# Two attention blocks placed head by head inside the projections that feed them

## The chip, the cores and the metric

One core of a Trainium2 chip. The metric is the device time of one execution in microseconds, the median of the runs shown. The kernel is written engine by engine: TensorE (PE) multiplies, VectorE (DVE), ScalarE (ACT) and GpSimd (POOL) work on elements, and SyncE (SP) issues the loads. Engines meet only at semaphores.

## What is computed

A transformer of three layers on 256 tokens of width 1024, in fp32. The change touches only the mixing part of the first layer:

```python
h = rms_norm(x, norm1_g[l])
parts = jnp.split(h @ w_in[l], list(SPLIT_POINTS), axis=-1)   # 2064 + 4608 columns
gq, gk, gv, gr, ga_lr = parts[:5]
log_a = jax.nn.log_sigmoid((ga_lr @ w_gla_a2[l] + b_gla_a[l]).astype(jnp.float32)) / GLA_TAU
o_gla = gla_chunked(heads(gq, GLA_DK), heads(gk, GLA_DK), heads(gv, GLA_DV), heads(log_a, GLA_DK))
o_gla = rms_norm(o_gla, gla_out_norm_g[l]).reshape(B, S, GLA_V_W) * jax.nn.silu(gr.astype(jnp.float32))
y_gla = o_gla.astype(x.dtype) @ w_proj_gla[l]
for gi, (window, dilation) in enumerate(DIL_PATTERNS):        # 3 groups, 4 heads of 128
    q, k, v = parts[5 + 3 * gi: 8 + 3 * gi]
    q = rms_norm(heads(q, DIL_DH), dil_q_norm_g[l, gi])
    k = rms_norm(heads(k, DIL_DH), dil_k_norm_g[l, gi])
    o_g, m_g, d_g = dilated_group(q, k, heads(v, DIL_DH), slopes[gi], window, dilation)
...
y_att = o_att.reshape(B, S, DIL_W).astype(x.dtype) @ w_proj_attn[l]
g_gla, g_att = jnp.split(jax.nn.sigmoid(h @ w_branch_gate[l] + b_branch_gate[l]), 2, axis=-1)
x = x + ((g_gla * y_gla + g_att * y_att) @ w_out[l]).astype(x.dtype)
```

GLA is a gated linear attention in chunks of 16 tokens with a running 128x128 state per head (4 heads, 16 chunks). The dilated attention is a softmax over three groups with different dilations. A mixture of 32 experts closes the first layer; two further layers follow.

## The kernel before, in words

**Stages.** The program is a list `stages` (from line 3217). Each stage gives every engine a function and ends at a barrier of all four (`end_stage`, line 439). The stages around the change are: norm `n1`, projection `in_a` (2064 columns: GLA's q, k, v, gate, and 16 decay columns last), `gla_*` (lines 959 to 1128), projection `in_b` (4608 columns), `dil_*` (1152 to 1274), projection `gates`, `y_gla`, `y_att` with the sum `sum_dve` (3173), a turn of the result, and `out_1`.

**Projections.** Weights stream in pieces of 128 x 2048 floats (1 MB) through a ring of nine slots (`stream`, 460, on SP's queue). ScalarE casts a piece to its rounded upper part (`split_high`, 554), VectorE subtracts to get the lower part (`split_low`, 560), and TensorE runs three matmuls per product of parts (`matmul3`, 536). A block of 512 columns is two pieces. Each piece is used for both tiles of 128 tokens, 24 matmuls of 512 columns in all; the y projections need one piece a block. `pe_project` (570) cycles through four PSUM banks, and `evacuate` (592) copies each finished tile out, on ScalarE for in_a and in_b, on VectorE for the others. Upper parts have four buffers. `pe_project` and `evacuate` have hooks, points at which a stage can put other work between pieces or between the two tiles of a piece; later layers use them.

**GLA stage.** Transposes of q and k of all heads, decay logits, logarithm and cumulative sums for all heads at once (1024 wide), scores, and then for each head and tile (`COMBOS`) a product of keys with masked values (`kv`, 985; POOL makes the 1024-wide masked values at 1126), a serial chain of state updates on VectorE (1100), and 16-column matmuls for the output (1005). Norm, gate and a turn for all heads end it.

**Dilated stage.** Squares, norms and scaling of q and k for all heads first (1225 to 1239), then head by head: 12 transposes (1160), scores (1167, 1169), bias, mask and maximum on VectorE (1250 to 1263), exponentials on ScalarE (1213, 1214), 9 transposes of the probabilities (1174, 1178), 9 matmuls with the values (1184, 1187), a division (1268).

Masks are built on VectorE between pieces of in_a (`masks_between`, 836), and rotary tables at its end (`rope_dve`, `rope_act`, called at 918 and in `params_wait`).

Of the kernel before, what the change touches and what calls it, by code (L numbers as in the profile page):

```python
# [117 lines left out]
def emit(nc, d, out):  # L118
    ctx = ExitStack()
    with ctx:  # L120
# [73 lines left out]
        gla_og = MT.take(GD)  # L194
        gla_a2 = MT.take(GW)[0:RANK]
# [29 lines left out]
        count_steps("gla_tensor", {"gla_turned": 3, "gla_logit": 1, "gla_scores": 1, "gla_ke_turned": 1,  # L225
                                   "gla_o_turned": 1, "gla_out": 1})
        count_steps("gla_scalar", {"gla_lr": 1, "gla_ln": 1, "gla_exp": 3, "gla_ke": 1, "gla_oT": 1, "gla_silu": 1,
                                   "gla_sq": 1, "gla_rt": 1, "gla_ogT": 1})
        count_steps("gla_vector", {"gla_y": 1, "gla_cum": 2, "gla_scaled": 1, "gla_att": 1, "gla_ms": 1, "gla_gated": 1})
# [43 lines left out]
        def new_piece(copies, group=None):  # L273
# [7 lines left out]
            p.copies = [(ring_flat[:, p.slot * PIECE + a:p.slot * PIECE + b], src) for a, b, src in copies]  # L281
            p.size = max(b for _, b, _ in copies)
# [6 lines left out]
        def project(name, weight, kc, width, engines, group, first=0, chunked=False):  # L289


            pieces_of[name], jobs_of[name] = [], []
            rows = weight.rearrange("(c p) n -> p c n" if chunked else "(p c) n -> p c n", c=kc)

            def jobs(p, col, n, off):
                for t in range(NT):
                    e = engines[len(jobs_of[name]) % len(engines)]
                    order[e] += 1
                    j = Job(t, col, n, off, e, order[e], len(jobs_of[name]))
                    p.jobs.append(j)  # L300
                    jobs_of[name].append(j)
# [10 lines left out]
            blocks = [(c0, min(512, width - c0)) for c0 in starts]  # L312
            if kc == PLE // P:
                p = new_piece([(0, PIECE, rows)], group)
                p.c0, p.chunks, p.width, p.last = 0, kc, width, True
                for c0, n in blocks:
                    jobs(p, c0, n, c0)
# [3 lines left out]
            for c0, n in blocks:  # L321
                chunks = kc if kc * n <= PIECE else kc // 2
                for c in range(0, kc, chunks):
                    p = new_piece([(0, chunks * n, rows[:, c:c + chunks, c0:c0 + n])], group)
                    p.c0, p.chunks, p.width, p.last = c, chunks, n, c + chunks == kc
                    pieces_of[name].append(p)
                    if c == 0:
                        jobs(p, c0, n, 0)
# [83 lines left out]
        group_a, group_b, group_c = [Group(4) for _ in range(3)]  # L412
        project("in_a", d["w_in"][0][:, 0:ZA], KC, ZA, ["act"], group_a)
        n_first = order["piece"]
        project("in_b", d["w_in"][0][:, ZA:ZA + ZB], KC, ZB, ["act"], group_b)
        project("gates", d["w_branch_gate"][0], KC, 2 * D, ["dve"], group_c)
        project("y_gla", d["w_proj_gla"][0], GW // P, D, ["dve"], group_c)
        project("y_att", d["w_proj_attn"][0], GW // P, D, ["dve"], group_c)
        project("out_1", d["w_out"][0], KC, D, ["dve"], group_c)
# [40 lines left out]
        def stream(sp, pieces):  # L460
            for p in pieces:
                if p.n >= RAW:
                    sp.wait_ge(used, p.n - RAW + 1)
                for dst, src in p.copies:
                    sp.dma_start(dst.rearrange("p (c n) -> p c n", n=src.shape[2]), src).then_inc(piece_ready[p.slot], 16)
# [104 lines left out]
        def pe_project(pe, name, xT, hook=None):  # L570
            hi, lo = xT
            jobs = jobs_of[name]
            for p in pieces_of[name]:
                pe.wait_ge(split, p.k)
                a, b = high_of(p, p.width), low_of(p, p.width)
                for j in p.jobs:
                    if p.c0 == 0 and j.q >= 4:
                        e = jobs[j.q - 4]
                        pe.wait_ge(evac_act if e.engine == "act" else evac_dve, e.evac)
                    cols, tok = slice(j.off, j.off + j.n), slice(j.tile * P, (j.tile + 1) * P)  # L580
                    for i in range(p.chunks):
                        c = p.c0 + i
                        mm = matmul3(pe, ps[:, j.q % 4, 0:j.n], hi[:, c, tok], lo[:, c, tok], a[:, i, cols], b[:, i, cols],
# [8 lines left out]
        def evacuate(eng, name, engine, copy=None, between=None, norm=None, hook=None):  # L592
# [7 lines left out]
            for i, p in enumerate(pieces_of[name]):  # L600
# [3 lines left out]
                if hook:  # L604
                    hook(eng, i, 0)
                for j in p.jobs if p.last else []:
                    if j.engine == engine:
# [3 lines left out]
                        copy(j, ps[:, j.q % 4, 0:j.n]).then_inc(evac_act if engine == "act" else evac_dve, 1)  # L611
                if hook:
                    hook(eng, i, 1)
# [134 lines left out]

        P1_LOADS = [
# [2603 lines left out]
```

## Time and profile before

| | us |
|---|---|
| median of 3 runs | 2638.46 (2633.21 to 2642.4) |
| the profiled execution | 2638.94 |
| its span, first to last instruction | 2637.2 |
| TensorE busy | 2360.6 (90%), mean clock 0.941 |
| VectorE busy | 1838.0 (70%) |
| ScalarE busy | 1451.2 (55%) |
| GpSimd busy | 56.5 (2%) |
| DMA | 617.66 MB, 234 GB/s on the mean |

The page cuts the span into 40 slices of 66 us. In the line of TensorE the first eight digits are 7, 6, 8, 9, 4, 6, 8, 7 where most others are 9, and the DMA line shows 0 in two of these slices. The mean over the span says little about this part; the windows by stage are the view to open.

### The profile page before, as it was taken

The numbers are of one execution on the slowest core, as the hardware profiler recorded it, in microseconds if no ns is written. First come the engines' busy times: TensorE is split into PE (matmuls) and PEld (weight loads), VectorE is DVE, ScalarE is ACT, GpSimd is POOL, SyncE is SP. The second block draws the span as 40 slices with busy tenths as digits, with TensorE's granted clock in tenths as the row PEclk, the third lists the DMA queues.
The fourth block names the chain that finished last, engine by engine and source line by source line (L and its number), as shares of the span: only waits on it lengthen the run. The fifth ranks groups of instructions, "written<-read, shape, count | busy, mean of one in ns | idle before, by whom it ended". The sixth has DMA issues, their size and how long they took to land. (4 is left out here: it accounts for less than half of the span.)

```text
span 2637.2 us, 30476 instructions
## 1 busy us (share of the span) xinstructions
PE 2360.6 (90%) x12398; PEld 1920.6 (73%) x12398; DVE 1838.0 (70%) x1869; ACT 1451.2 (55%) x1357; POOL 56.5 (2%) x47
## 2 busy tenths in 40 slices
PE   7689468799999999797899989779999999999996
PEld 6567356678888888676688768557888888888884
DVE  5443544588888898476555447657888888888884
ACT  4243123477777777443534444346767767767763
POOL 0200000000000000011000001000000000000000
PEclk9789678899999999898999999889999999999997
DMA  7025024399999999630555444127999998999990
GB/s 261 32 99 188 0 74 136 110 345 367 359 368 356 368 357 370 208 105 19 162 175 192 166 130 142 33 72 279 363 358 357 366 361 291 363 357 357 367 327 29
DMA packets 232601, 617.66 MB, mean 234 GB/s; under 512 B 23289, under 2 KB 68729, under 8 KB 194817
## 3 DMA queue, kind: packets, MB, share of 16 engines
q1 hardware_dynamic: 231056, 611.39, 65.4%
q10 hardware_dynamic: 1392, 4.19, 0.4%
q8 instruction: 102, 1.67, 0.2%
q14 instruction: 51, 0.41, 0.1%
HBM read 612.40 MB, written 1.05 MB: 233 GB/s over the span
## 5 line engine op out<-in xcount | busy, mean ns | idle before, releaser
L562 DVE TENSOR_TENSOR ring_parts<-ring,high_parts 128x2048 fp32r<-128x2048 f32 x574 | 1282.1, 2274 | 219.6 <-ACT high_parts L558 198.6
L558 ACT CAST high_parts<-ring 128x2048 fp32r<-128x2048 f32 x574 | 1078.5, 1897 | 259.7 <-PE ps L540 226.1
L540 PE MATMUL ps<-high_parts,arena_parts 128*128 128x512 f32 (+2 forms) x1560 | 620.4, 398 | 0.0
L538 PE MATMUL ps<-high_parts,hT_parts 128*128 128x512 f32 (+2 forms) x1120 | 451.9, 403 | 38.8 <-DVEq L442 23.5
L539 PE MATMUL ps<-ring_parts,hT_parts 128*128 128x512 f32 (+2 forms) x1120 | 445.2, 397 | 0.0
L538 PE MATMUL ps<-high_parts 128*128 128x512 f32 x912 | 365.4, 401 | 0.0
L539 PE MATMUL ps<-ring_parts,high_parts 128*128 128x512 f32 x912 | 359.2, 394 | 0.0
L540 PE MATMUL ps<-high_parts 128*128 128x512 f32 x912 | 356.6, 391 | 0.0
L540 PEld LDWEIGHTS ps<-high_parts,arena_parts 128*128 128x128 f32 x1560 | 299.3, 192 | 69.1
L538 PE MATMUL ps<-high_parts,arena_parts 128*128 128x512 f32 x744 | 295.4, 397 | 11.7 <-ACTq L442 4.5
L539 PE MATMUL ps<-ring_parts,arena_parts 128*128 128x512 f32 x744 | 294.0, 395 | 0.0
L538 PEld LDWEIGHTS ps<-high_parts,hT_parts 128*128 128x128 f32 x1120 | 216.7, 194 | 90.3 <-DVEq L442 26.0
L539 PEld LDWEIGHTS ps<-ring_parts,hT_parts 128*128 128x128 f32 x1120 | 216.9, 194 | 49.6 <-issue 0.2
L540 PEld LDWEIGHTS ps<-high_parts 128*128 128x128 f32 x912 | 171.5, 188 | 41.8
L538 PEld LDWEIGHTS ps<-high_parts 128*128 128x128 f32 x912 | 172.1, 189 | 37.5
L539 PEld LDWEIGHTS ps<-ring_parts,high_parts 128*128 128x128 f32 x912 | 171.0, 188 | 35.7
L538 PEld LDWEIGHTS ps<-high_parts,arena_parts 128*128 128x128 f32 x744 | 140.8, 189 | 46.0 <-ACTq L442 4.9
L539 PEld LDWEIGHTS ps<-ring_parts,arena_parts 128*128 128x128 f32 x744 | 141.0, 190 | 32.5
L2075 DVE SCALAR_TENSOR_TENSOR arena<-ps,arena 128x512 f32<-128x512 f32 x80 | 57.8, 722 | 149.3 <-PE ps L540 134.1
L1991 ACT CAST arena_parts<-ps 128x512 fp32r<-128x512 f32 x80 | 45.4, 567 | 140.4 <-PE ps L1889 140.4
L540 PE MATMUL ps<-high_parts,hT_parts 128*128 128x512 f32 x304 | 120.5, 397 | 0.0
L2009 ACT ACTIVATE arena<-ps 128x512 f32<-128x512 f32 x80 | 46.2, 578 | 68.6 <-PE ps L540 68.6
(523 smaller groups left out, 1867.4 us busy)
## 6 DMA issues: line engine op xcount, KB each, us to landing
ring<-in_moe_w SPq DMA_DIRECT2D x248, 1024.0 KB, 5.5
ring<-in_w_gate SPq DMA_DIRECT2D x64, 1024.0 KB, 5.3
ring<-in_w_up SPq DMA_DIRECT2D x64, 1024.0 KB, 5.2
ring<-in_w_down SPq DMA_DIRECT2D x64, 1024.0 KB, 5.2
ring<-in_w_in SPq DMA_DIRECT2D x46, 1024.0 KB, 4.9
ring<-in_ffn_w SPq DMA_DIRECT2D x44, 512.0 KB, 4.8
ring<-in_moe_w SPq DMA_DIRECT2D x32, 512.0 KB, 5.0
ring<-in_w_out SPq DMA_DIRECT2D x12, 1024.0 KB, 4.9
```

What stands on the lines that cost most here:

```text
L538: pe.matmul(dst, a_hi, b_hi, start=first, stop=False, skip_group_check=True)
L539: pe.matmul(dst, a_hi, b_lo, start=False, stop=False, skip_group_check=True)
L540: return pe.matmul(dst, a_lo, b_hi, start=False, stop=last, skip_group_check=True)
L558: act.copy(high_flat(p), raw_flat(p)).then_inc(upper, 1)
L562: dve.tensor_tensor(raw_flat(p, ring_parts_flat), raw_flat(p), f32(high_flat(p)), ALU.subtract).then_inc(split, 1)
L1991: act.copy(m_hidT[:, 0:st.n // P, :].rearrange("p c n -> p (c n)"), ps[:, TURN, 0:st.n])\
L2009: act.activation(m_sg[:, 0:st.n], ps[:, GATE, 0:st.n], ACT.Silu).then_inc(sig("moe_silu"), 1)
L2075: dve.scalar_tensor_tensor(out=m_hid[:, 0:st.n], in0=src, scalar=m_gate[:, q:q + 1], in1=m_sg[:, 0:st.n], op0=ALU.mult, op1=ALU.mult).then ...
```

## The change

The two projections in_a and in_b become one, `in_ab`. Its blocks are the 16 decay columns first, then four blocks that each hold q, k, v and gate of one GLA head, then nine blocks with the dilated columns ordered by head (q and k of the three groups, then v). A piece of such a block is loaded by one copy for each 128 columns. in_ab, gates, y_gla and y_att form one stage. They use two PSUM banks in turn (0 and 1), which leaves six for attention, and three buffers of upper parts. The attention steps hang on hooks at fixed slots; slot 2p is behind the first tile of piece p, slot 2p + 1 behind the second. The lists G_TURN to D_PV name the slots.

Smaller changes: state products work on two halves of 64 rows with masked values 512 wide; output norm and gate are computed per head on transposed data, with the sum of squares by a matmul with ones; the silu is built from an exponential and a reciprocal; bias and mask are added up ahead and a single instruction does addition and minimum; the probabilities are turned by a matmul with a diagonal of 1/sum; the sigmoid is a tanh, with its 1/2 applied in `out_copy`; some masks are made earlier; the rotary tables move to piece 31.

```diff
+        for what, engine in (("turned", "tensor"), ("scores", "tensor"), ("hi", "scalar"), ("lo", "vector")):
+            count_steps(f"{what}_{engine}", {f"g_{what}": GH, f"d_{what}": DH})
...
+                    j.bank = len(lanes[name]) % banks
+                    j.before = lanes[name][-banks] if len(lanes[name]) >= banks else None
...
-                    p = new_piece([(0, chunks * n, rows[:, c:c + chunks, c0:c0 + n])], group)
+                    p = new_piece([(0, chunks * n, rows[:, c:c + chunks, c0:c0 + m], n, at) for (c0, m), at in zip(part, places)], group)
...
-        group_a, group_b, group_c = [Group(4) for _ in range(3)]
-        project("in_a", d["w_in"][0][:, 0:ZA], KC, ZA, ["act"], group_a)
...
+        group_m = Group(3)
+        in_blocks = [[(4 * GW, RANK)]] + [[(k * GW + h * GD, GD) for k in range(4)] for h in range(GH)]
+        dil_cols = [(ZA + (3 * g + k) * GW + h * DD, DD) for h in range(DH)
+                    for k, g in [(k, g) for g in range(DG) for k in range(2)] + [(2, g) for g in range(DG)]]
+        in_blocks += [dil_cols[i:i + 4] for i in range(0, len(dil_cols), 4)]
+        project("in_ab", d["w_in"][0], KC, ZA + ZB, ["act"], group_m, blocks=in_blocks, banks=2)
+        project("gates", d["w_branch_gate"][0], KC, 2 * D, ["dve"], group_m, banks=2, after="in_ab")
...
-                    if p.c0 == 0 and j.q >= 4:
-                        e = jobs[j.q - 4]
+                    if p.c0 == 0 and j.before:
+                        e = j.before
                         pe.wait_ge(evac_act if e.engine == "act" else evac_dve, e.evac)
...
+        G_TURN, G_SCORES, G_KV, G_OUT, G_MS = [[a + 4 * h for h in range(GH)] for a in (8, 10, 12, 15, 17)]
+        D_TURN, D_SCORES, D_PTURN, D_PV = [28, 37, 46, 57], [31, 40, 49, 60], [34, 43, 52, 64], [37, 46, 55, 67]
...
+            def gla_kv(h):
+                pe.wait_ge(sig("g_att"), h + 1)
+                if h:
+                    pe.wait_ge(sig("g_state"), h)
+                for t in range(NT):
+                    pe.wait_ge(sig("g_vm"), NT * h + t + 1)
+                    for f in range(2):
+                        rows = slice(64 * f, 64 * f + 64)
+                        mm = pe.matmul(bank(4 + 2 * t + f), g_ke[rows, t, :], g_vm[rows, t].rearrange("p n v -> p (n v)"),
+                                       start=True, stop=True)
+                mm.then_inc(sig("g_kv"), 1)
+
+            def gla_out(h):
+                pe.wait_ge(sig("g_state"), h + 1)
+                if h:
+                    pe.wait_ge(sig("g_og"), h)
...
+            def dil_turn(h):
+                pe.wait_ge(sig("d_normed"), h + 1)
...
+        def first_act(act):
+            def logit_act():
+                act.wait_ge(*ended("g_logit", 1))
...
+                astep(act, act.activation(flat(g_abs), flat(g_abs), ACT.Exp, scale=-1.0))
+                act.activation(flat(g_abs), flat(g_abs), ACT.Ln, bias=1.0).then_inc(sig("g_ln"), 1)
...
+            def hook(act, i, phase):
...
+                    if i == 2:
+                        logit_act()
...
+                    if i == 31:
+                        rope_act(act)
+                    return
+                if i == 3:
+                    decay_act()
...
+                    if i == G_MS[h] // 2:
+                        act.wait_ge(sig("g_ms"), h + 1)
+                        act.activation(g_e, ps[:, 2, S:2 * S], ACT.Sqrt, scale=1.0 / GD, bias=eps_c).then_inc(sig("g_rt"), 1)
...
+            def gla_states(h):
+                dve.wait_ge(sig("g_kv"), h + 1)
+                for n in range(NT * NCH - 1):
...
+            def gla_silu(h):
+                dve.wait_ge(sig("g_sq"), h + 1)
+                vstep(dve, dve.tensor_scalar(g_e, g_e, 1.0, None, ALU.add))
+                vstep(dve, dve.reciprocal(g_e, g_e))
...
+            def gla_gate(h):
+                dve.wait_ge(sig("g_rt"), h + 1)
+                vstep(dve, dve.reciprocal(g_e, g_e))
...
+            def dil_squares(h):
+                after_block(dve, keys_block(h))
...
+                vstep(dve, dve.tensor_tensor(d_sq[h], qk, qk, ALU.mult))
+                dve.tensor_reduce(d_ss, d_sq[h], AX, ALU.add).then_inc(sig("d_ms"), 1)
...
+            def dil_max(h):
+                dve.wait_ge(*ended("d_scores", h + 1))
+                dve.tensor_tensor_reduce(out=d_s[:, 0:DG * P].rearrange("p (g n) -> p g n", g=DG),
...
+        def first_mix_pool(pool):
+            for h in range(GH):
+                after_block(pool, 1 + h)
...
+                    pool.tensor_tensor(g_vm[:, t], g_za[h][:, 2, t, :].unsqueeze(1).to_broadcast([P, 4, GD]),
...
+        def out_copy(dve, j, src):
+
+            cols = x[:, j.tile, j.col:j.col + j.n]
+            return dve.scalar_tensor_tensor(out=cols, in0=src, scalar=0.5, in1=cols, op0=ALU.mult, op1=ALU.add)
...
+            (first_pe, first_act, first_dve, first_mix_pool),
             stage_turn("ym", c_y, low_1),
...
-            stream(sp, pieces_of["in_a"][0:6])
+            stream(sp, pieces_of["in_ab"][0:3])
+            for dst, src in G_LOADS:
+                sp.dma_start(dst, src).then_inc(sig("g_params"), 16)
+            stream(sp, pieces_of["in_ab"][3:7])
```

`keys_block(h)` is the block with which the last of a dilated head's q and k arrive (6, 8, 10 and 13); VectorE squares them at piece 12, 16, 20 and 26 and normalizes at the next.

## Rows read from the trace of the kernel before

**Rows 1.** Windows by stage: length; PE, PEld, DVE, ACT, POOL busy us; clock; DMA share; GB/s.

```profile
17.20:72.60 55.40, 55.34 (x240) 45.86 (x240) 31.91 (x101) 20.03 (x22) 0.00 (x0) 0.90 0.70 226
72.60:153.70 81.10, 46.01 (x235) 35.02 (x235) 42.47 (x86) 23.75 (x26) 15.08 (x8) 0.71 0.04 14
153.70:258.30 104.60, 103.77 (x432) 83.03 (x432) 38.83 (x18) 43.73 (x35) 0.00 (x0) 0.97 0.52 171
258.30:367.90 109.60, 44.52 (x212) 39.24 (x212) 54.66 (x92) 22.27 (x41) 0.00 (x0) 0.67 0.03 10
```

**Rows 2.** Timeline of VectorE, last sums: start us, us, engine, line, operation.

```profile
445.02 2.36 DVE L3176 TENSOR_TENSOR arena<-arena 128x1024 f32<-128x1024 f32 x2
```

**Rows 3.** Timeline of ScalarE and VectorE in the in_b projection.

```profile
176.22 0.69 ACT L3182 ACTIVATE arena<-ps,rstd 128x512 f32<-128x512 f32 x1 [0.83 <-PE ps L540]
...
179.62 1.89 ACT L558 CAST high_parts<-ring 128x2048 fp32r<-128x2048 f32 x1
...
187.45 0.69 ACT L3182 ACTIVATE arena<-ps,rstd 128x512 f32<-128x512 f32 x1 [0.85 <-PE ps L540]
...
175.42 2.29 DVE L562 TENSOR_TENSOR ring_parts<-ring,high_parts 128x2048 fp32r<-128x2048 f32 x1 [2.80 <-ACT high_parts L558]
```

**Rows 4.** Timeline of TensorE, the 48 matmuls of the 16-column block.

```profile
64.73 0.17 PE L538 MATMUL ps<-high_parts,hT_parts 128*128 128x16 f32 x1
...
67.32 0.35 PE L538 MATMUL ps<-high_parts,hT_parts 128*128 128x16 f32 x1
...
72.21 0.36 PE L540 MATMUL ps<-high_parts,arena_parts 128*128 128x16 f32 x1
```

**Rows 5.** Windows after the restart of TensorE at 153.7.

```profile
156.00:160.00 4.00, 4.00 (x12) 3.17 (x11) 4.00 (x2) 3.17 (x2) 0.00 (x0) 0.56 0.00 0
160.00:164.00 4.00, 4.00 (x19) 3.21 (x18) 2.37 (x2) 1.73 (x1) 0.00 (x0) 1.00 0.17 35
```

**Rows 6.** Timeline of TensorE, the second dilated head.

```profile
303.25 1.47 PE L1160 MATMUL ps<-ident,arena 128*128 128x128 f32 x12
306.13 0.91 PE L1167 MATMUL ps<-arena 128*128 128x128 f32 x6 [1.41 <-ACT arena L1210]
306.88 1.46 PE L1169 MATMUL ps<-arena 128*128 128x256 f32 x6
```

**Rows 7.** Timeline of TensorE in the GLA stage.

```profile
120.64 1.96 PE L991 MATMUL ps<-arena 128*128 128x512 f32 x4
...
126.39 1.63 PE L1005 MATMUL ps<-arena 128*128 128x16 f32 x14
```

**Rows 8.** Timeline of TensorE, 64-row matmuls in a later layer.

```profile
1130.98 0.48 PE L2344 MATMUL ps<-arena 64*128 64x256 f32 x1
1130.99 0.48 PE L2345 MATMUL ps<-arena 64*128 64x256 f32 x1
1131.30 0.38 PE L2344 MATMUL ps<-arena 64*128 64x256 f32 x1
```

**Rows 9.** Timeline of VectorE in the GLA and dilated stages.

```profile
83.39 1.66 DVE L1057 TENSOR_SCALAR arena<-ps,gla_bT 128x256 f32<-128x256 f32 x4 [3.36 <-PE ps L971]
...
109.45 5.54 DVE L1100 SCALAR_TENSOR_TENSOR arena<-arena,ps 128x128 f32<-128x128 f32 x14
...
258.26 1.23 DVE L1228 TENSOR_TENSOR arena<-arena 128x1024 f32<-128x1024 f32 x1 [18.37 <-ACTq L442]
```

**Rows 10.** Groups of VectorE, reciprocals: count, busy us, mean ns.

```profile
L3058 DVE RECIPROCAL arena<-arena 128x60 f32<-128x60 f32 x2 | 1.1, 528 | 0.1
...
L1233 DVE RECIPROCAL arena<-arena 128x48 f32<-128x48 f32 x1 | 0.5, 452 | 0.3 <-ACT arena L1203 0.3
```

**Rows 11.** DMA over 1261 to 1400, loads of 1 KB rows: GB/s in 40 slices.

```profile
GB/s 164 365 405 348 257 78 226 205 110 289 127 182 0 0 0 0 90 363 150 5 54 342 362 147 0 68 339 365 137 0 97 322 363 124 0 94 336 362 118 0
```

**Rows 12.** Timeline of ScalarE, first dilated head.

```profile
285.49 1.28 ACT L1213 ACT_TABLE_LOAD   x1
294.46 0.61 ACT L1213 ACTIVATE arena<-arena 128x384 f32<-128x384 f32 x1 [7.70 <-DVE arena L1263]
```

More of the change, by code:

```diff
@@ L280, in new_piece @@
             p.ready = piece_val[p.slot]
-            p.copies = [(ring_flat[:, p.slot * PIECE + a:p.slot * PIECE + b], src) for a, b, src in copies]
-            p.size = max(b for _, b, _ in copies)
+            p.copies = []
+            for a, b, src, *part in copies:
+                width, at = part or (src.shape[2], 0)
+                rows = ring_flat[:, p.slot * PIECE + a:p.slot * PIECE + b].rearrange("p (c n) -> p c n", n=width)
+                p.copies.append((rows[:, :, at:at + src.shape[2]], src))
+            p.size = max(c[1] for c in copies)
             if group:
@@ new lines, in emit @@
+        g_za = [v[:, 0:4 * S].rearrange("p (k t e) -> p k t e", k=4, t=NT) for v in g_head]
+        g_up, g_down, g_end = [[v[:, (4 + k) * S:(5 + k) * S] for v in g_head] for k in range(3)]
+        g_qT = [MA.take(S) for _ in range(2)]
+        g_kT, g_yk = [MA.take(S) for _ in range(2)]
+        g_att = [MA.take(NT, P) for _ in range(2)]
+        g_ke = MA.take(NT, P)
+        g_vm = MA.take(NT, 4, GD)
+        g_st = MA.take(NT * NCH, GD)
+        g_sq, g_e, g_sil, g_og = [MA.take(S) for _ in range(4)]
@@ new lines, in emit @@
+        d_z = [MB.take(9, NT, DD) for _ in range(2)]
+        d_qk = MB.take(2, DG, S)
+        d_sq = [d_z[1].rearrange("p k t e -> p (k t) e")[:, 0:6 * NT]] + 3 * [d_qk.rearrange("p k g s -> p (k g s)").rearrange("p (n e) -> p n e", e=DD)]
+        c_late = [MB.take(NT, 512)]
+        d_s = MB.take(9 * P)
+        d_pT = MB.take(9, P)
+        d_bias = MB.take(DG, S)
+        d_diag = MB.take(NT, P)
+        c_bias = MB.take(2 * D)
+        d_max, d_den, d_rd = [MB.take(NT) for _ in range(3)]
@@ new lines, in emit, with block_jobs, after_block @@
+        MB.at = MA.at
+        d_ss, d_rt = [MB.take(6 * NT) for _ in range(2)]
+        assert MB.at <= group_m.high_at
+        MB.at = b1_at
+        c_early = [MB.take(NT, 512) for _ in range(2)]
+        MB.at = b1_at + 9 * S
+        c_gate = c_early + c_late + [MB.take(NT, 512)]
+        c_y = MB.take(NT, D)
+        MB.at = b1_at + 4 * 7 * S
+        c_t = MB.take(NT, D)
+        def block_jobs(b):
+            return jobs_of["in_ab"][2 * b:2 * b + 2]
+        def after_block(eng, b):
+            eng.wait_ge(evac_act, block_jobs(b)[-1].evac)
```

787 lines of the change are left out of this document (397 added, 390 removed).

## The prediction, made before the change was run

> **What bounds the kernel now.** I read the windows by stage first. Of the 430.2 us from the first projection matmul (17.2) to the last sum (447.4) [rows 1, 2], 190.7 are the two attention stages: TensorE is busy for 46.0 of 81.1 and 44.5 of 109.6 us there, mostly at the lower clock (mean 0.71 and 0.67), and DMA stands at 0.04 and 0.03. No engine is full in them; each is a chain of waits. The projection beside them (153.7 to 258.3) is the opposite: TensorE 103.8 of 104.6, VectorE 38.8, ScalarE 43.7. Its rhythm stands in the timeline: one block of 512 columns every 11.2 us, two pieces of 5.6, four slots of 2.8 us a block. A piece takes 1.89 us of cast from ScalarE and 2.29 of subtraction from VectorE [rows 3]. So each piece leaves some 3.5 us free on either engine, and the attentions could live there. Whatever the later stages need is already in the ring, so time saved before 447.4 is saved in full.
>
> **The change, part by part.** The end of the y_att sums is the sum's goal: 447.4 before.
>
> 1. Projections: 26 pieces of in_ab, 8 of gates, 4 of y: 38 x 5.6 = 212.8 us. Arithmetic and bytes are the same.
>
> 2. The 16-column block goes first. It has 48 matmuls. In the trace they took 0.11 us each at the full clock and 0.213 when it had fallen: it fell 2.6 us into the block, though TensorE never paused [rows 4]. First after an idle stretch, I put all 48 at half (1.2 of 2.4 GHz): 48 x 0.213 = 10.2. Its small piece needs no 1.9 us cast and no 2.3 us subtraction, so TensorE starts at some 13.6, not 17.2. The following dense piece still pays the restart: 5.7 us at half the clock in the windows, so 2.9 lost [rows 5].
>
> 3. Attention work put between projection slots. A GLA head: 4 transposes 0.5 (12 take 1.47 [rows 6]); two score matmuls at 0.25 each (three take 0.74 [rows 6]) and two transposes, 0.75; the state products, below; the output, two 128-wide and 15 of 16 columns at 0.23 (seven in 1.63; an fp32 matmul shows as two records [rows 7]) with two transposes, 4.2; one 256-wide sum of squares 0.45. **State products**: before, 4 matmuls of 512 columns at 0.93 = 3.7 a head (two take 1.86 [rows 7]). Now the four work on 64 rows each, in pairs on different halves. Elsewhere such a pair starts 0.01 us apart and runs side by side [rows 8]. So the bounds are 1.8 (pairs overlap) and 3.7 (they don't); I take 1.8, the row of the same shape of operand. GLA: 7.7 x 4 = 30.8, and 2.4 for the decay logits. A dilated head: 12 transposes 1.5, scores 0.74 + 1.46 = 2.2 [rows 6], nine turns of the probabilities, now real matmuls against a diagonal, 2.2, nine value matmuls 2.2: 8.1 x 4 = 32.4. Together 65.6.
>
> TensorE alone: 13.6 + 10.2 + 2.9 + 212.8 + 65.6 = 305.1, then 0.7 for the last eviction and 1.4 for two sums: 307.2.
>
> 4. **Stalls.** I laid each head's chain on the slots. With two PSUM banks a tile must be evicted within 2.8 us of TensorE's next use, and ScalarE's queue is in order, so whatever waits ahead of an eviction stops TensorE.
>  - Start. ScalarE's four absolute values 1.5, two table loads 2.6 and two 1024-wide functions 2.1 stand ahead of block 1's eviction: 4.2 late. The decay (subtraction 1.23, four scans 2.44, differences 1.66, exponentials 3.1) stands ahead of block 2's: 2.5 late.
>  - GLA heads. VectorE per head: two subtractions 4.5, scaling 1.2 and masking 0.8 (0.41 per 256 columns), the state chain 15 x 0.396 = 5.9 [rows 9], reciprocals of 256 columns, twice, products 2.1, masks for later 1.6. A 60-wide reciprocal takes 0.528 us and a 48-wide one 0.452 [rows 10], so 0.0063 a column: 1.8 each, an estimate. The sum is 19.7 against TensorE's 11.2 + 7.7 = 18.9. The loop that binds (norm of head h-1, output 4.2, exponential 0.8, silu 2.5, subtraction 2.2, scaling 1.2, states 5.9, norm 2.6) is 19.4. Late by 0.7, 0.7, 0.5 and, with the dilated squares (1536 columns, 1.8 twice by the 1.23 for 1024 [rows 9]) close behind, 2.9: 4.8.
>  - Turn to the dilated part: VectorE has states, norm, squares, masks (2.3), silu and the first normalization in one row; the first transpose waits 5.9.
>  - Dilated heads: 0.5 at the first scores; the eviction of block 8 behind the exponentials and a cast, 2.5; the second head's turn waits for maximum 1.6, an eviction, a table load 1.3, exponentials 1.9, cast 1.9, subtraction 2.3, diagonal 0.7 against 8.4 of slots, 3.2. The other two heads fit.
>  - Gates: 0.8 at the last turn, 2.0 because the rotary tables (VectorE 1.6, ScalarE's sine and its load) now stand before an eviction.
>  Sum 4.2 + 2.5 + 4.8 + 5.9 + 3.0 + 3.2 + 2.8 = 26.4, goal at 333.6.
>
> 5. Entering and leaving projection: 31 visits. The first matmul of a kind shows 0.48 in place of 0.38 [rows 8], so 0.1 each way: 6. Bounds 0 and twice that.
>
> 6. **Clock.** The output's 15 small matmuls in a row, 3.5 us, are like the narrow block in which the clock fell though TensorE never paused [rows 4]; against that, in the stage of before short runs of them stood between wide ones and the clock held. A fall costs up to 2.9 [rows 5]. Bounds: 0, and 12 falls (four outputs, eight stalls over 2 us) at 2.9, with the rest of each output at half the clock (1.6), 41. I take four at 2.5: 10.
>
> 7. Costed at nothing. POOL builds two 512-wide products a head and has 20 us for them; without that cover each is about 1 us. SP issues four copies a piece instead of one; a small load's issue takes it 0.43 us, so 1.7 a piece, under 5.6. Rows of 512 bytes: with 1 KB rows the queue reached 366 GB/s [rows 11], so a row costs at most 1024 B / (366/16 GB/s) = 45 ns on its engine, and a piece of 2048 rows between 2.8 and 5.8 us; TensorE takes one in (212.8 + 65.6)/38 = 7.3 on the mean. Three small loads go before piece 3, the other 18 after piece 6; both are awaited 10 us after they can have landed. The bias load and the tanh in place of one sigmoid lie beside gates. The halved residual copy costs 0.05.
>
> 8. Table loads. The chain shows one load at 1.28, started ahead of the wait of the function it serves [rows 12]. The change alternates exponential and square root in every head, sixteen loads more, of which four are exposed and counted above. The Trainium skill (ScalarE: Activation LUTs, "What ACT_TABLE_LOAD costs" and "Table sets") adds a drain of 1.38 to each switch and advises against such alternation; by it the sum would be 4 x 1.38 = 5.5 higher, and no such gap stands behind the loads of this trace.
>
> Sum: 333.6 + 6 + 10 = 349.6, which is 97.8 before 447.4. The profiled execution took 2638.9 (span 2637.2 and 1.7 around it), 0.5 over the median: 2638.9 - 97.8 = **2541**.
>
> **Rivals.**
>  - *The clock falls often*: item 6 at its upper bound, 31 more: 2572. For it: the narrow block [rows 4]. Against it: the mixed stretch of the old GLA, at 1.00.
>  - *Transposes let it fall as well*, at the eight visits that transpose q and k: 8 x 2.9 = 23 on top, 2595. Against it: 12 transposes right behind matmuls took 0.12 each, and the scores after them ran at the full rate [rows 6]. The Trainium skill (TensorE: Matmul & The Clock Gate, Part 4: PE-mode transpose) states that a transpose doesn't count as busy in the way a matmul does; no row here tests it by itself.
>  - *VectorE becomes the bound*: it has 0.8 us more than TensorE a GLA head already. If its queue runs 3 us longer a head (reciprocals steeper than the estimate, semaphore hops in the 60-step chains) and the dilated stalls double: 12 + 9 = 21, 2562. With state products that don't overlap, 7.6 more.
>  - *Slower than before*: the interleaving trades one stage's chain for 31 places where TensorE itself stops, with two banks and in-order queues. If every visit waited as ScalarE once waited for VectorE in the old dilated chain, 7.7 us [rows 12], the sum is 31 x 7.7 - 97.8 = 141 slower, 2780. It decides from 3.2 us a visit beyond the 0.9 that I count.
>  - *It doesn't interleave*: a wait in a queue that only the projection's end fulfils gives the old order, about 2638. The order of slots shows none.
>
> **How the numbers follow.** Forecast 0.62, clock 0.15, transposes 0.03, VectorE 0.10, better than the forecast's own range (no falls, half the stalls, under 2515) 0.05, no interleaving 0.02, slower 0.03. The forecast's range is 2515 to 2567, from items 4 to 6 at their ends; the range to hold 8 in 10 takes in the clock and VectorE rivals: 2515 to 2590. This kernel's measurement can tell 0.3% (8 us) from no change. Faster 0.96, same 0.01, slower 0.03.
>
> **What would show it.** In the windows of the changed kernel, 14 to 350 should have TensorE over 90% busy at a clock over 0.9; the small block first, with 0.21 between matmuls; pairs of state products 0.01 apart; periods of some 20 us between GLA outputs; the longest TensorE waits on VectorE's first normalization and on the two early evictions; the sums ending near 350, and everything behind them unchanged in length. It is wrong if a GLA period is over 24, if the clock in 24 to 300 is under 0.85, or if SP's copies land after TensorE wants them.

## The result and the profile after the change

| | before | after |
|---|---|---|
| median | 2638.38 us (4 runs) | 2521.59 us (4 runs, 2518.11 to 2523.52) |
| span of the profiled execution | 2637.2 | 2520.0 |
| TensorE busy, mean clock | 2360.6, 0.941 | 2343.5, 0.962 |
| VectorE busy | 1838.0 | 1843.8 |
| end of the y_att sums | 447.4 | 329.6 |

The ratio is 0.9557, with a 95% interval of 0.9537 to 0.9577. The prediction was 2541 with a range of 2515 to 2590: the direction and the mechanism were right, and the kernel came out 19 us faster than the number.

The two profile pages first. The span fell by 117.2 us, and the sums of y_att end 117.8 earlier, so the part behind them is 0.6 us longer than before: what was saved ahead of the sums was saved in full. These lines are from the page of the kernel after: engines, then slices of 63 us.

```profile
PE 2343.5 (93%) x12426; PEld 1909.0 (76%) x12426; DVE 1843.8 (73%) x1898; ACT 1462.2 (58%) x1382; POOL 49.6 (2%) x47
...
PE   7999978999999997978999897879999999999996
...
PEclk9999989999999998989999898989999999999998
```

In the first eight slices before stood a 4, two 6s and two 7s; here the first and the sixth are 7 and the others 8 or 9. Then the windows of the kernel after, by stage, with the same columns as [rows 1]: the 16-column block, the decay, the GLA heads, the first half of the dilated heads, the rest up to the sums.

```profile
13.60:24.00 10.40, 10.22 (x48) 10.25 (x49) 7.16 (x17) 7.19 (x9) 0.00 (x0) 1.00 1.20 287
24.00:65.00 41.00, 36.94 (x143) 28.90 (x144) 23.98 (x53) 22.82 (x24) 2.04 (x2) 0.92 0.90 212
65.00:145.00 80.00, 78.64 (x404) 62.85 (x403) 69.76 (x138) 32.39 (x36) 6.14 (x6) 0.94 0.45 119
145.00:250.00 105.00, 98.44 (x482) 81.72 (x481) 63.65 (x90) 53.68 (x65) 0.00 (x0) 0.97 0.44 131
250.00:335.00 85.00, 78.78 (x381) 64.22 (x380) 55.13 (x70) 39.77 (x41) 0.00 (x0) 1.00 0.49 161
```

Before, the two attention stages had TensorE busy for 46.0 of 81.1 and 44.5 of 109.6 us [rows 1]; now it is busy for 78.64 of 80 in the GLA heads. VectorE is busy for 69.76 of the same 80, which is the second number to keep in mind.

Third, the timeline of TensorE after, each step on which an expectation rested. A bracket is the idle time before a row and what ended it.

```profile
13.78 0.35 PE L554 MATMUL ps<-high_parts,hT_parts 128*128 128x16 f32 x1 [3.93 <-DVE ring_parts L578]
...
44.13 0.76 PE L554 MATMUL ps<-high_parts,hT_parts 128*128 128x512 f32 x1 [4.07 <-ACT arena L1151]
...
67.87 1.99 PE L1032 MATMUL ps<-arena 64*128 64x512 f32 x8
...
78.94 0.38 PE L1041 MATMUL ps<-arena 128*128 128x128 f32 x2
...
97.88 0.46 PE L1041 MATMUL ps<-arena 128*128 128x128 f32 x2
...
121.92 1.86 PE L1043 MATMUL ps<-arena 128*128 128x16 f32 x16
...
139.15 0.46 PE L1041 MATMUL ps<-arena 128*128 128x128 f32 x2 [1.36 <-DVE arena L1307]
...
141.24 3.06 PE L1043 MATMUL ps<-arena 128*128 128x16 f32 x16
...
150.75 1.53 PE L1066 MATMUL ps<-ident,arena 128*128 128x128 f32 x12 [1.42 <-DVE arena L1325]
...
209.59 3.90 PE L1086 MATMUL ps<-arena 128*128 128x128 f32 x18 [2.84 <-DVE arena L1354]
```

L1032 are the state products (four matmuls, eight records, 1.99 us: the pairs overlap), L1041 the wide matmuls that open each half of a head's output, L1043 the 16-column matmuls of a half, L1066 the first turn of the dilated part, L1086 the turned probabilities of the second dilated head. The last sums, as in [rows 2]:

```profile
328.32 1.28 DVE L1424 TENSOR_TENSOR arena<-arena 128x512 f32<-128x512 f32 x2
```

The clock was at its lower level behind the wait of 4.07 us at 44, fell twice inside a head's output (at 100 and at 141, in the second and fourth heads: the same half takes 3.06 us at 141 and 1.86 at 122), and was at the lower level again behind the 2.84 at 210. These are the windows of the fall at 100, and of the third head beside it:

```profile
100.00:104.00 4.00, 4.00 (x23) 3.81 (x22) 2.40 (x12) 0.71 (x3) 0.00 (x0) 0.59 0.77 213
104.00:108.00 4.00, 4.00 (x13) 3.11 (x12) 3.93 (x4) 1.73 (x1) 0.00 (x0) 0.56 0.00 0
120.00:124.00 4.00, 4.00 (x38) 4.00 (x37) 3.73 (x11) 0.47 (x1) 0.00 (x0) 1.00 0.68 175
```

The third head has the same work at 120 as the second at 98, and kept its clock.

### The profile page after: what moved, and what is told of

It reads as the page before. It is cut to its first block and busy times, and to the rows that moved or that the text cites. A ratio compares the mean times of both kernels' runs of the same rounds, so it can differ in the third digit from the quotient of the medians.

```text
span 2520.0 us, 30651 instructions
## 1 busy us (share of the span) xinstructions
PE 2343.5 (93%) x12426; PEld 1909.0 (76%) x12426; DVE 1843.8 (73%) x1898; ACT 1462.2 (58%) x1382; POOL 49.6 (2%) x47
## 3 DMA queue, kind: packets, MB, share of 16 engines
q8 instruction: 103, 1.69, 0.3%
## 5 line engine op out<-in xcount | busy, mean ns | idle before, releaser
L578 DVE TENSOR_TENSOR ring_parts<-ring,high_parts 128x2048 fp32r<-128x2048 f32 (+1 forms) x574 | 1282.6, 2275 | 193.1 <-ACT high_parts L574 179.8
L574 ACT CAST high_parts<-ring 128x2048 fp32r<-128x2048 f32 (+1 forms) x574 | 1079.1, 1897 | 222.2 <-PE ps L556 194.8
```

Of the source, the lines that this page charges most:

```text
L574: act.copy(high_flat(p), raw_flat(p)).then_inc(upper, 1)
L578: dve.tensor_tensor(raw_flat(p, ring_parts_flat), raw_flat(p), f32(high_flat(p)), ALU.subtract).then_inc(split, 1)
```

## The experiments

All are edits of the kernel after, and each is read at two places: the end of the y_att sums in its profile (329.6 in the kernel after), and its time. The first leaves out the part behind the sums, which none of the edits touches and which yet varies: it takes 2186.7 to 2190.4 us in the profiles of the kernels with right values, and 2184.5 in that of experiment 1, whose values are off, so that other experts may be chosen later. But each end stands in one profiled execution alone. Against the medians, the two readings of a change agree within 1.3 us in eight experiments, within 2.7 in 11 and 12 and within 2.2 in 6, and differ by 5.4 in experiment 1.

**1. Do the pairs of state products overlap, and does TensorE's time count?**

```
-    rows = slice(64 * f, 64 * f + 64)
+    rows = slice(0, 64)
```

> The 16 state products of the GLA heads all read partitions 0 to 63 (the output is not the reference's), so two neighbours can't run side by side. Theory (TensorE is the bound and the pairs overlap): four products take about 3.7 us a head in place of 1.99, the sums of y_att end 6 to 8 us later than 329.6, and the time is 2528 to 2530. Rival A (the pairs never overlapped, one matmul of 64 rows is simply cheap): rows and time unchanged. Rival B (VectorE sets the pace of the GLA heads and TensorE has slack): rows at 3.7, but under 3 us at the end.

2524.19 us, where I expected 2528 to 2530. The sums end at 337.6, 8.0 later, as expected; the part behind them is 5.9 us shorter in this profile, and the cause of that is not shown.

```profile
68.65 3.70 PE L1032 MATMUL ps<-arena 64*128 64x512 f32 x8
...
158.03 2.82 PE L1066 MATMUL ps<-ident,arena 128*128 128x128 f32 x12 [4.49 <-DVE arena L1325]
```

The row goes from 1.99 to 3.70 us, and 4 x 1.7 = 6.8 of the 8.0 are that. So the overlap is real, and in the profile it is counted in full. The Trainium skill (TensorE: Matmul & The Clock Gate, Part 3: Packing small matmuls — row/col tiling) says that small matmuls on different parts of the array run at the same time; 1.99 against 3.70 agrees. One reading must be corrected at once, though: TensorE still waits for VectorE before the first dilated turn, 4.49 us. TensorE has slack at that point, so its load alone can't be the reason for the 8.0. The products stand in the chain of each head, between the turned keys and the states, and so they also hold up VectorE, which works on the states.

**2. The narrow matmuls of the output, twice.**

```
     for t in range(NT):
+        for _ in range(2):
             pe.matmul(bank(2, t * P, P), g_za[h][:, 2, t, :], ...
             for n in range(NCH * t + (t == 0), NCH * (t + 1)):
                 pe.matmul(bank(2, n * GCH, GCH), g_st[:, n, :], ...
```

> The output matmuls of each GLA head (2 of 128 columns, 15 of 16) are issued twice. Theory (a run of narrow matmuls lets the clock fall even where TensorE never pauses): the granted clock falls at all four heads in place of two; 3.5 us a head at the full clock is 14, the second pass at half clock adds about 1.6 a head and two more falls 2.2 each: 22 to 26 us, 2544 to 2548. Rival A (the falls at heads 1 and 3 came from the waits before them): still two falls, 14 to 16 us. Rival B (VectorE sets the pace): under 10 us.

2545.29 us; the sums end at 354.3, 24.7 later. The clock now falls in the output of all four heads, at full TensorE activity:

```profile
80.00:84.00 4.00, 4.00 (x38) 4.00 (x37) 0.39 (x2) 0.00 (x0) 0.00 (x0) 1.00 0.86 218
84.00:88.00 4.00, 4.00 (x21) 4.00 (x21) 0.00 (x0) 0.00 (x0) 0.00 (x0) 0.51 0.17 48
...
112.00:116.00 4.00, 4.00 (x21) 4.00 (x20) 0.00 (x0) 0.00 (x0) 0.00 (x0) 0.50 0.03 7
...
140.00:144.00 4.00, 4.00 (x20) 4.00 (x21) 0.12 (x1) 0.00 (x0) 0.00 (x0) 0.50 0.00 0
...
168.00:172.00 4.00, 4.00 (x16) 3.61 (x16) 1.01 (x2) 1.73 (x3) 0.00 (x0) 0.50 0.00 0
```

There is no wait ahead of any of them, from 44 to 175 us. The clock falls in a run of 16-column matmuls though TensorE never pauses, and rival A is out. That the longer run makes the falls more frequent is not shown: in experiment 11 the clock falls at all four heads with the output as it was.

**3 to 5. The GLA stretch as two bounds.** Four kernels in a square: with and without the 15 matmuls of 16 columns, with and without the two reciprocals on VectorE.

```
-    for n in range(NCH * t + (t == 0), NCH * (t + 1)):
-        pe.matmul(bank(2, n * GCH, GCH), g_st[:, n, :], ...
```

> The 15 matmuls of 16 columns of each GLA head are left out (the output lacks the part of the carried states). Theory: both falls near 100 and 141 us are gone; TensorE has 3.1 us less a head, 12.6, and 4.4 less of low clock, 17 in all, but VectorE, with 69.8 of 80 us busy there, then sets the pace at some 17.5 to 19 us a head: new TensorE waits on VectorE, and 8 to 12 us gained, 2510 to 2514. Rival A (TensorE alone is the bound): 17 us, 2505. Rival B (VectorE's 19.3 us of work a head is already the bound): under 4 us. Rival C (the falls come from the waits): the clock still falls near 100 and 141.

```
-    vstep(dve, dve.reciprocal(g_e, g_e))
+    vstep(dve, dve.tensor_scalar(g_e, g_e, 1.0, None, ALU.mult))
```

> The two reciprocals of 256 columns of each GLA head (1.75 us each) are replaced by products with 1 (0.29 each; the output is not the reference's): 2.9 us less on VectorE a head, TensorE's work unchanged. Theory (before the first normalization TensorE and VectorE's chain are within a few us of each other, so that low clock of TensorE and waits on VectorE stand in for one another): the waits on VectorE at 139 and 151 go, 2.8 us, the falls stay, and the sums end 2 to 5 us before 329.6. Rival (VectorE alone sets the pace): 4 x 2.9 = 11.7 us earlier. Rival (TensorE alone): 0 to 1.

> Both left out: the GLA reciprocals and the 15 matmuls of 16 columns of each head. Leaving out the matmuls alone gained 4.1 of the 17 us that TensorE had less. Theory (two near-equal bounds): with VectorE relieved as well most of the 17 us appears: 13 to 17 us before 329.6, clearly more than the two gains alone added up. Rival (the 13 us went to something else than VectorE's work in the GLA heads, such as ScalarE's evictions or the loads): the two gains only add up, 6 to 9 us.

| | first dilated turn | wait there | sums end | gain |
|---|---|---|---|---|
| the kernel after | 150.75 | 1.42 | 329.6 | |
| no narrow matmuls (2517.25 us) | 145.07 | 7.89 | 325.5 | 4.1 |
| no reciprocals (2515.70 us) | 146.37 | 0 | 323.8 | 5.9 |
| neither (2506.74 us) | 135.02 | 5.88 | 314.7 | 14.9 |

Without the narrow matmuls no fall is left inside an output; the two falls of the stretch now stand behind the waits of 3.43 and 7.89, so rival C of experiment 3 is out.

Timeline of TensorE without the narrow matmuls:

```profile
113.20 0.68 PE L1041 MATMUL ps<-arena 128*128 128x128 f32 x4 [1.61 <-DVE arena L1304]
120.33 3.10 PE L1032 MATMUL ps<-arena 64*128 64x512 f32 x8 [3.43 <-DVE arena L1277]
...
145.07 2.82 PE L1063 MATMUL ps<-ident,arena 128*128 128x128 f32 x12 [7.89 <-DVE arena L1322]
```

and with neither:

```profile
135.02 2.82 PE L1063 MATMUL ps<-ident,arena 128*128 128x128 f32 x12 [5.88 <-DVE arena L1322]
```

Taking 12.6 us of narrow matmuls and two falls of the clock (17 in all) from TensorE gains 4.1, because waits on VectorE of 14.5 us stand there (1.08 + 1.61 + 3.43 + 0.53 + 7.89), where the kernel after has 2.8. The two reciprocals of 1.75 us, made 0.29, are 11.7 us less on VectorE and gain 5.9, just over the 2 to 5 that I expected. Both gain 14.9, which is 4.9 more than the two added up. So in the GLA heads TensorE's row of work and the chain through VectorE are near-equal bounds; low clock of the one and waits on the other stand in for each other. I had put the gain of the first at 8 to 12, and it was 4.1: nearer to rival B. Whether VectorE's part is its load or the length of the chain can be read from windows of VectorE. The first two are the periods between outputs without the narrow matmuls, the last is the kernel after between its last output and the first dilated turn:

```profile
94.60:113.20 18.60, 15.91 (x75) 11.65 (x75) 17.83 (x38) 8.93 (x11) 3.69 (x2) 1.00 0.45 118
113.20:133.50 20.30, 16.34 (x65) 11.16 (x65) 19.32 (x39) 8.85 (x10) 0.00 (x0) 0.92 0.37 101
...
139.15:150.75 11.60, 10.18 (x49) 8.83 (x49) 11.32 (x26) 5.16 (x8) 0.00 (x0) 0.71 0.31 89
```

VectorE is busy for 17.83 of 18.60, 19.32 of 20.30 and 11.32 of 11.60 us. The loop through an output, 19.4 by the prediction, would be some 16 with 3.1 less of output, an estimate; the periods are longer. So it is the load that binds there, and part of it has no place in any head's chain: from 115.2 to 119.2 VectorE makes masks for later, with the copy that TensorE waits for (L1277) queued behind them.

**6. GLA heads not interleaved inside.**

```
-    ... for a in (8, 10, 12, 15, 17)]
+    ... for a in (9, 9, 9, 9, 9)]
```

(with the state products ahead of the output in the slot, and some masks made earlier)

> The five steps of each GLA head stand in one slot between projection matmuls, each waiting for the one before; the columns are still ordered by head and the dilated part is interleaved as before. Some masks are made earlier. Theory (the gain is the interleaving): TensorE stands still in each head through scaling 1.3, masking 0.8, states 5.6, squares and silu 3.3, some 11 us, and restarts at half the clock, 2.2: 4 x 13 = 52, less the waits of the GLA stretch that go: the time is 2565 to 2575. Rival (the gain came from the column order and from filling the time between the stages, so that VectorE's work can catch up in the next block): under 25 us.

2591.14 us, 69.6 over the kernel after and 16 over what I expected; the sums end at 401.4, 71.8 later. Timeline of TensorE, first head:

```profile
64.14 1.22 PE L1019 MATMUL ps<-arena 128*128 128x128 f32 x4 [5.37 <-DVE arena L1273]
...
66.64 3.78 PE L1032 MATMUL ps<-arena 64*128 64x512 f32 x8 [0.85 <-DVE arena L1279]
76.18 0.79 PE L1041 MATMUL ps<-arena 128*128 128x128 f32 x2 [5.76 <-DVE arena L1288]
76.77 3.01 PE L1043 MATMUL ps<-arena 128*128 128x16 f32 x14
...
87.54 1.19 PE L1052 MATMUL ps<-arena,ones 128*128 128x256 f32 x2 [3.41 <-DVE arena L1299]
```

The waits are 11.2 to 15.4 us a head, 51.2 in all, where I had some 11 a head, 44. What I had left out is that the clock is at half between waits that stand so close. L1032 takes 3.78 in place of 1.99, the 14 records of L1043 3.01 in place of some 1.6. So breaking up each head's chain is worth 71.8 us of the 117.8 in the GLA stretch alone. The dilated part was not tried by itself, so how the other 46 us are shared out is not shown.

**7. One copy a piece.**

```
-    p = new_piece([(0, chunks * n, rows[:, c:c + chunks, c0:c0 + m], n, at) for (c0, m), at in ...], group)
+    p = new_piece([(0, chunks * n, rows[:, c:c + chunks, part[0][0]:part[0][0] + n], n, 0)], group)
```

> Each piece of in_ab is loaded by one copy of 512 neighbouring columns (rows of 2 KB, the wrong columns, so the output is not the reference's) in place of four copies with rows of 512 bytes. Theory (item 7: loads and issues are hidden): the DMA share of these stretches falls to about the half, and the sums end within 1 us of 329.6. Rival (the short rows or SP's four issues hold up pieces somewhere): 3 us or more earlier, most of it before 60 us, where the DMA share stands at 1.2.

2520.64 us; the sums end at 329.3, as expected. The DMA share of 24 to 65 falls from 0.90 to 0.55, and the time doesn't change. Rows of 512 bytes and four issues a piece are hidden.

**8. The output in two slots.**

```
-    if slot == G_OUT[h]:
-        gla_out(h)
+    if slot in (G_OUT[h], G_OUT[h] + 1):
+        gla_out(h, slot - G_OUT[h])
```

> The output of a GLA head is made in two halves, 1.6 and 1.9 us long, with a slot of dense matmuls (2.8 us) between them. Theory (a long run of narrow matmuls lets the clock fall; in the GLA stretch VectorE is the floor, as leaving the narrow matmuls out gained 4 of 17 us): no fall, or a shorter one, near 100 and 141, but the squares and the silu come 2.8 us later in the chain, so the sums end between 2 us earlier and 4 us later. Rival A (the falls are on the path): 4 us earlier. Rival B (a fall depends on what came before, not on the length): falls as before.

2533.40 us; the sums end at 342.6, 13.0 later, three times the upper end of what I expected. Timeline of TensorE:

```profile
100.36 0.77 PE L1040 MATMUL ps<-arena 128*128 128x128 f32 x2 [3.01 <-DVE arena L1306]
...
125.26 0.46 PE L1040 MATMUL ps<-arena 128*128 128x128 f32 x2 [3.00 <-DVE arena L1306]
...
147.79 0.77 PE L1040 MATMUL ps<-arena 128*128 128x128 f32 x2 [3.07 <-DVE arena L1306]
```

L1306 ends the gate of the head before: an output waits until the bank is read out by it, and that read waits for squares and silu, now 2.8 us later. Three waits of 3.0 where the kernel after has one of 1.36, and 5.25 for 1.42 before the dilated turn, make 11.5 of the 13.0. As to the clock: at 100 and at 148 it is at half from the end of the wait on, and in the third head it falls behind the first half, at 127, 1.9 us after the wait. In the first head, which has no wait, it held at 1.00 from 76 to 92, but so it did there in the kernel after with the output in one run. So this experiment doesn't show that a shorter run keeps the clock.

**9. ScalarE's decay work behind the eviction.**

```
-    if i == 2:
-        logit_act()
...
+    if i == 2:
+        logit_act()
```

(from phase 0 of piece 2, ahead of the eviction, to phase 1, behind it)

> ScalarE's absolute values, exponential and logarithm of the decay (6.5 us with two table loads) come behind the eviction of block 1 in its queue, not ahead of it. Theory: the wait of 4.07 us at 44 and the half clock after it (2.5) go, but the decay's three exponentials now stand ahead of the eviction of block 2, so a wait of 3 to 5 us appears near 52 to 56, and the first GLA head starts no earlier: the sums of y_att end 0 to 3 us before 329.6. Rival (no other work is in the way): the whole 6.6 us are gained, 2515.

2526.47 us; the sums end at 335.8, 6.2 later, where I expected 0 to 3 earlier.

```profile
59.78 0.76 PE L554 MATMUL ps<-high_parts,hT_parts 128*128 128x512 f32 x1 [8.59 <-ACT arena L1151]
```

The wait of 4.07 went, and one of 8.59 came for the next eviction, behind the decay's exponentials. That it moves there was expected (3 to 5 us), its size was not: TensorE arrives some 6.6 us earlier, and the exponentials end at 57.3, 1.8 later than in the kernel after, since the logarithm now waits for an eviction.

**10. Two waits behind 150 us.**

```
-    [34, 43, 52, 64]      (slots of the turned probabilities)
+    [34, 44, 52, 64]
```

(and the rotary tables in the second phase of the same piece)

> The rotary tables come behind the eviction of their piece on VectorE and ScalarE, and the second dilated head's turned probabilities one slot later (44 for 43). Behind 170 us VectorE has slack, so theory: the waits of 1.69 at 292 and of 2.84 at 210, and the half clock after the second (1.2), go and nothing takes their place: the sums end 4 to 5.7 us before 329.6, 2516 to 2518. Rival (the wait moves to the next step that needs the same work, the turned probabilities' copy or the next eviction): under 2 us.

2518.06 us; the sums end at 326.9, 2.7 earlier, under the 4 to 5.7 expected. The wait of 2.84 is gone and nothing took its place. The one of 1.69 stayed, to the hundredth: piece 31 has no eviction, so the second phase of it is no later than the first; what holds up the gates' eviction in piece 32 is that ScalarE's cast stands behind a sine that waits for VectorE's angles. The first dilated turn came at 150.24, with falls at 84 and 122 in place of 100 and 141, and a wait of 4.37: the turn's time hardly depends on which heads lost their clock.

```profile
150.24 2.82 PE L1066 MATMUL ps<-ident,arena 128*128 128x128 f32 x12 [4.37 <-DVE arena L1325]
```

**11 and 12. Versions from these readings.** The first (e10_four_moves) puts the logarithm behind the eviction of block 1 and the exponentials behind that of block 2, gives ScalarE the squares of the first dilated head, and moves the turned probabilities and the rotary tables (34 for 31).

```
+    if i == 2:
+        logit_act()
+    if i == 4:
+        decay_act()
+    if i == 12:
+        act.activation(d_sq[0], d_z[0][:, 0:6]..., ACT.Square).then_inc(sig("d_sq"), 1)
```

> Four moves together: the decay's logarithm behind the eviction of block 1 and its three exponentials behind that of block 2; the squares of the first dilated head on ScalarE (VectorE loses 1.75 us just ahead of the first normalization); the second head's turned probabilities one slot later; the rotary tables behind the last piece of gates. Theory: the waits of 4.07, 2.84 and 1.69 go, a wait of some 2.4 at the first scores takes the place of the first, and the floor that VectorE sets ahead of the first normalization comes 1.75 earlier: 4 + 1.7 + 2.7 + 1.7 = 10 before 329.6, 2511. Rival (VectorE's chain of the GLA heads starts as late as before, because the decay is on it): only the moves behind 150 us pay, 4 to 6, 2516. A wait for the squares on ScalarE would show as a later eviction near 135.

2513.71 us; the sums end at 324.4, 5.2 earlier, half of the 10. The waits at 44, 210 and 292 went, but the first scores waited 5.00 in place of 2.4, and the rotary tables held an eviction at 305 for 2.02. Their scaled operands were ready at 59.2, where the kernel after, with its wait of 4.07, has them at 60.6: the chain began only 1.4 us earlier. The clock falls at all four heads here, at 82, 103, 124 and 144, with no wait ahead of the first three. Two of the four in windows:

```profile
84.00:88.00 4.00, 4.00 (x17) 2.90 (x18) 3.96 (x3) 1.83 (x2) 0.00 (x0) 0.75 0.01 3
...
124.00:128.00 4.00, 4.00 (x13) 2.87 (x13) 3.93 (x8) 2.10 (x3) 0.00 (x0) 0.63 0.14 41
```

The next version goes for the start of VectorE's chain.

```
-    if i == 3:
-        decay_dve()
...
     if i == 2:
         logit_dve()
+        decay_dve()
```

(with the absolute values ahead of the eviction again, and the rotary angles at piece 25)

> e10_four_moves with two moves more: the decay's subtraction and scans on VectorE follow the logits at once, not behind the low part of the next piece (which waits for ScalarE's cast, and that for the eviction of block 1), with the absolute values ahead of that eviction again; and the rotary angles are computed nine pieces before the sines, so that VectorE and ScalarE no longer wait for each other at the last piece of gates. Theory (VectorE's chain of the GLA heads is the floor, and its start is set by the decay): the wait of 5.00 us at the first scores shrinks to some 2, the wait of 2.02 at 305 goes, and the sums of y_att end 4 to 5 us before the 324.4 of e10_four_moves; 2509. Rival (the floor isn't the start of the chain but what VectorE does between the last GLA head and the first normalization): only the 2.0 of the rotary tables, 2512.

2509.63 us (5 runs, 2507.31 to 2512.99), ratio to the kernel before 0.9519 (0.9505 to 0.9533); the sums end at 320.3, 4.1 before those of the version above and 9.3 before those of the kernel after. Timeline of TensorE:

```profile
57.32 0.71 PE L1019 MATMUL ps<-arena 128*128 128x128 f32 x4 [1.80 <-DVE arena L1282]
```

The wait of 5.00 shrank to 1.80, though one of 1.36 came at 52, and the one of 2.02 at 305 is gone. The operands of the first scores and the first dilated turn both come 1.9 us earlier than in the version above: the start of VectorE's chain was a floor, and it is worth 1.9 of the 4.1. This is the fastest version; of the 12.0 us between the medians 9.3 are these.

## Why the prediction was right, and where it was off

The prediction said 349.6 for the end of the sums, and the trace says 329.6. The measured time lies 6.6 us above the lower end of its range. By its own steps:

1. **Projections.** The 912 dense matmuls of the 38 pieces took 0.233 us each at the full clock: 212.7 against 212.8.
2. **Small block.** Start 13.78 (13.6), length 10.2 (10.2), restart 2.4 (2.9).
3. **Attention work: 58.5 at the full clock against 65.6, the second term that was mis-sized.** From the start of each group to the start of what follows, a GLA head takes 7.2 (7.7) and a dilated head 6.9 (8.1). I had added up durations of rows, which hold the tail of the last matmul: the three 256-wide scores last 1.46 in [rows 6], but in the kernel after the next work starts 1.11 after their start. The overlap of the state products, taken at 1.8 between bounds of 1.8 and 3.7, is 1.9 from start to start, and experiment 1 shows it.
4. **Stalls: 13.9 against 26.4, the term that failed.** The wait behind ScalarE's decay work is there (4.07 for 4.2), and so are those of the dilated heads and the gates (7.0 for 9.0). But the 2.5 for the eviction of block 2 did not come, the 4.8 of the GLA heads came as 1.36, and the 5.9 at the turn to the dilated part as 1.42: 10.4 of the 12.5. I had laid VectorE's chain beside a TensorE that runs at full clock, found it late by these amounts, and then added the low clock of item 6 on top. A TensorE that comes late finds VectorE ready, or nearly so. Behind the wait of 4.07 and its restart it was 6.5 us late, and block 2 had been evicted, 0.4 us before; with that lateness taken away (experiment 9) a wait appears there, and of 8.59. Ahead of the first dilated turn the low clock from 141 on stands where the wait would have stood: 1.42 here, 4.37 in experiment 10, the turn at 150.75 and at 150.24.
5. **Entering and leaving**: the dense matmuls lost 14.1 us over their full rate. The start took 2.4 of them, three falls 6.7 (2.5, 2.2, 2.0), and 5.0 are left for 31 visits, 0.16 each, where I had 6 in all.
6. **Clock**: those 6.7, and 4.0 in the attention's own matmuls (the second half of an output 2.6 and 2.9 in place of 1.7, the probabilities' turn behind the wait at 210 3.6 for 1.9): 10.7 against 10, four falls against four. The size was right, in part by luck, since experiment 7 has five falls with the same TensorE code (behind 44, 84, 104, 126 and 150); that it was an addition was not right.
7. **Costed at nothing**: the loads are, by experiment 7, and POOL's products never ended a wait of TensorE.
8. **Table loads**: no extra pause stands behind a load in the trace (last section).

Together: 12.5 less in stalls, 7.1 less in attention work, 0.5 in the restart and 1.0 in the visits, 0.7 more of low clock and 0.2 at the start, 20.2 in all, for the 20.0 between 349.6 and 329.6. The two large terms erred the same way, so the number was not saved by errors that cancel. One of its signs failed with the fourth: the longest waits were to be those for the first normalization and for the two early evictions; one of these evictions cost nothing, and the wait for the normalization (1.42) is shorter than the one for the probabilities (2.84).

Of the rivals, VectorE as the bound came nearest: experiments 3 to 5 show that it is one of two. I had worked out 19.7 us a head for its load, 19.4 for its loop and 18.9 for TensorE; between outputs the periods are 18.9, 22.0 and 19.2, with VectorE busy for 18.2 of the last. It cost nothing beyond the forecast, because its waits and the low clock of TensorE stood in for each other. *Transposes let it fall*: the Trainium skill (TensorE: Matmul & The Clock Gate, Part 4: PE-mode transpose) says that a transpose doesn't count as busy in the way a matmul does. In this trace the 12 transposes at 186 and 224 took 1.47 at the full clock, with no fall behind them, and no run here shows such a cost. *Slower* and *no interleaving* are out by the time and the windows. Experiment 6 shows what carries the gain: 71.8 of 117.8 us come from the steps of a GLA head standing in different slots.

## What to carry over

When two engines are near-equal bounds, their delays may not be added. Lay both rows of work out, take the later one at each meeting point, and put a clock loss into TensorE's row before comparing; then look for the wait it has swallowed. In VectorE's row count all its work, that for later stages too, and not only the chain. And where a wait is removed by reordering an in-order queue, find what stands behind in the same queue: experiments 9 and 11 moved a wait on, and 12 gained 1.9 us more by an earlier start of the other engine's chain.

## What the runs showed of the hardware that was not expected

- The clock fell in or right behind two of four equal outputs of 3.5 us, narrow matmuls for the most part, with TensorE busy throughout. Over the eight kernels that keep the interleaving and this output (the kernel after and experiments 1, 4, 7, 9 to 12) it fell at 19 of 32 heads, from two to all four of a kernel; with the output twice as long (experiment 2), at four of four. Which heads it hit differed from kernel to kernel (100 and 141 here; 84, 104 and 126 in experiment 7, whose TensorE code is the same), so a single head tells nothing. What decides it is not shown.
- The granted clock in the records can be off. In the kernel after, the windows from 14 to 24 say 1.00 while the 16-column matmuls took 0.213 us each, the half rate; in experiment 1 the same block of 10.2 us is recorded at 0.50.

```profile
16.00:20.00 4.00, 4.00 (x21) 4.00 (x20) 2.38 (x3) 3.95 (x6) 0.00 (x0) 1.00 1.20 290
```

  The duration is the surer witness.
- A table load costs its own 1.28 us and no more. Timeline of ScalarE after, two loads in a row of the decay:

```profile
41.06 1.28 ACT L1175 ACT_TABLE_LOAD   x1
42.35 1.06 ACT L1175 ACTIVATE arena<-arena 128x1024 f32<-128x1024 f32 x1
```

  The function follows 0.01 us behind the load. The Trainium skill (ScalarE: Activation LUTs, "What ACT_TABLE_LOAD costs") adds a drain of some 1.38 us to it; this trace shows none, and the 5.5 us that it would have put on the sum are not there.
